# A mixer's hand-written order changed in three places: abs ahead of relu, low parts of turned blocks ahead of the softmax scaling, mean products a half projection behind their squares

## The chip, the core and the metric

The kernel runs on one core of a Trainium2 chip. Five engines run their own instruction streams and meet through semaphores: PE (TensorE: matrix products and turnings), ACT (ScalarE), DVE (VectorE), POOL (GpSimd) and SP (issues most DMAs). The metric is the device time of one execution in microseconds (us).

## What is computed

One encoder layer for one sequence of 512 positions and width 1024, in float32:

```python
h = modulate(x, g_ffn1, shift0, scale0);  x = x + 0.5 * gate0 * swiglu(h, w_ffn1_up, w_ffn1_down)
h = modulate(x, g_mix, shift1, scale1);   proj = h @ w_in          # q k v of 16 heads of 64, gates, forget logits
# 8 stick-breaking heads: z = q k^T / 8
log_beta = log_sigmoid(z); log_keep = where(strict, log_beta - z, 0)
w = where(strict, exp(log_beta + suffix_sum(log_keep)), 0);   o_sb = rmsnorm(w @ v)
# 8 forgetting heads: q, k = rmsnorm(q), rmsnorm(k)
p = softmax(where(causal, q k^T / 8 + f_cum[q] - f_cum[k], -inf));  o_fx = rmsnorm(p @ v) * sigmoid(gate)
x = x + gate1 * (concat(o_sb, o_fx) @ w_out)
h = modulate(x, g_ffn2, shift2, scale2);  x = x + 0.5 * gate2 * swiglu(h, w_ffn2_up, w_ffn2_down)
return rmsnorm(x, g_final)
```

## The kernel before

Every float32 product is made of three products of rounded parts: a high part (`_hi`, written by ACT) and the rest (`_lo`, written by DVE as value minus high part). So each weight tile of 128x1024 costs ACT one `w_hi` (L1107) and DVE one `w_lo` (L1471), and each product on PE is `three` (L694 to L696). Raw tiles arrive in four slots `w_raw`; SP loads a slot again once `w_lo_done` says that it was read. Split tiles have two slots.

The program is: first feed-forward block, mixer, output projection, second feed-forward block, final norm. The change lies in the mixer. It has eight jobs j of two heads: jobs 0 to 3 stick-breaking, 4 to 7 forgetting. A job has five units u of packed score blocks (128 x 512). A unit (j, u), numbered 5j+u, goes through these steps:

- `scores` on PE, into bank 2 or 3 (`bank[2 + unit % 2]`).
- `prep`. Stick-breaking: relu of the scores on DVE into `tmp_b` (L1839), and on ACT abs into `tmp_a` (L1374), exp (L1376), ln (L1378). Forgetting: on DVE the row maximum (L1849, negated at L1855), then on ACT the softmax exp with row sums (L1388).
- `sum`. Stick-breaking: on DVE the reversed scans (L1867) and a subtraction (L1871), then `exp` on ACT (L1394). Forgetting: reciprocal (L1878) and scaling (L1882) on DVE.
- `turn`: four 128x128 transposes on PE into bank 4 or 5 (L984).
- `unload`: high part `pt_hi` on ACT (L1402), low part `pt_lo` on DVE (L1889).
- `values`: once per job and head, the products of the turned blocks with v into bank 6 (L694 to L696 with `pt_hi` or `pt_lo` among the operands). Head 0 of job j is made in period u = 4 of job j, head 1 in period u = 1 of job j+1.

Beside them run the projections (`proj`, two halves per weight tile, 12 products 512 wide or 24 products 256 wide each), their evacuation (`evac`: q, k or v into high and low parts, or a gate's sigmoid in three ACT passes, L1303 to L1307), the splitting of weight tiles (`split`), the row of forget sums (`decay`, L1021 on PE, L1366 on ACT, through bank 7), and a chain of four steps per head norm: `square` on ACT into `ssum` (L1331); `stat`, the mean product on PE into bank 7 (L1012) with ln and exp on ACT (L1338, L1340); `scale` on DVE (L1804, for gated outputs L1809 too); `part`, high part on ACT (L1349, L1356, L1358) and low part on DVE (L1816, L1823, L1827). There are 16 norms: outputs of jobs 0 to 7, and q and k of jobs 4 to 7. Only one chain moves at a time.

The order of all this is fixed before the program is built, by `mixer_steps`. It walks through the 40 units; for each it runs through a string of letters, a period: `PERIOD[0]` for stick-breaking, `PERIOD[1]` for forgetting units. S is scores, P prep, U sum, E exp, T turn, L unload (T and L of the unit before), v values, d and D decay, a a half projection, b more of them if due, x the pending splits, m one step of the oldest norm chain, t one evacuation and one chain step. `LAG_STAT` holds a `stat` back until PE has been given so much work since the square; a half projection counts 12, scores 4, a turning 2. All engines then walk through the same list `STEPS`, each issuing its own part of every step, so the list sets the order within each engine; waits on semaphores set the rest.

Of the kernel before, what the change touches and what calls it, by code (L numbers as in the profile page):

```python
# [22 lines left out]
SBJ = 4  # L23
# [57 lines left out]

PERIOD = ("StPaamUdamvbtDTxxLxE", "SmPdaabTvtUtEamxDL")


LAG_STAT, LAG_BANK, LAG_TILE = 4, 1, 5
BEHIND = 18


# [5 lines left out]
def mixer_steps():  # L96
# [37 lines left out]
    def tick(force=False):  # L134

        if evacs:
            for b in banks_of(evacs[0][1]):
                since[b] = spent[0]
            emit(*evacs.pop(0))
        move(force)  # L140
# [75 lines left out]
    for p, (j, u) in enumerate(units):  # L216
        before = units[p - 1] if p else None
        due = min(total, halves_due(p))
        while u == 0 and any(step in made_first(j) for step in evacs + [chain[-1] for chain in chains]):
            tick(True)  # L220
        for item in PERIOD[0 if j < SBJ else 1]:
            if item == "S":
# [57 lines left out]
def hybrid_block_kernel(  # L280
# [4 lines left out]
    with ctx:  # L285
        def sem(name):
            return ctx.enter_context(nc.semaphore(name))
# [14 lines left out]
        def keep(name, shape, dt=F32):  # L302
# [127 lines left out]
        s_done, relu_done, abs_done, eneg_done, e_ready, scan_done, d_ready, p_ready_sb = (  # L430
            sem("s_done"), sem("relu_done"), sem("abs_done"), sem("eneg_done"), sem("e_ready"),
            sem("scan_done"), sem("d_ready"), sem("p_ready_sb"))
# [40 lines left out]
        def turned(u):  # L473

            if u in (0, 4):
                return [(u // 4, slice(3, 13, 3), slice(0, 4))]
            if u in (1, 3):
                return [(u // 3, slice(2, 9, 3), slice(0, 3)), (u // 3, slice(0, 1), slice(3, 4))]
            return [(0, slice(1, 5, 3), slice(0, 2)), (1, slice(1, 5, 3), slice(2, 4))]

        def blocks(b, which):
            return b[:].rearrange("p (b n) -> p b n", n=P)[:, which, :]
# [10 lines left out]
        def chunk_read(ci):  # L493

            what, n, _, _ = CHUNKS[ci]
            if what == "v":
                return v_ready, 2 * n + 2
            if what == "g":
                return g_copy, n - SBJ + 1
            if n < SBJ:  # L500
                return qk_ready, 2 * n + 1 + int(what == "k")
            return nrm_f32, norm_of(what, n) + 1
# [10 lines left out]
        def z_read(unit):  # L513

            return (d_ready, unit + 1) if unit < 5 * SBJ else (max_done, unit - 5 * SBJ + 1)
# [85 lines left out]
        def _(sp):  # L601
# [55 lines left out]
            for kind, n, _, tile in CHUNKS:  # L657
                if kind == "v":
                    c0 = (2 if n < 2 else 5) * 512 + (n % 2) * 256
                    for part in range(2):  # L660
                        t = tile + part
                        load_w(t, t % RAW, tile4(w_raw, t % RAW), in_v[:, 4 * part:4 * part + 4, c0:c0 + 256])
                else:
                    c0 = (3 * 512 if n >= SBJ else 0) + (n % SBJ) * P + {"q": 0, "k": 512, "g": 3 * 512}[kind]
                    load_w(tile, tile % RAW, tile8(w_raw, tile % RAW), in_v[:, :, c0:c0 + P])
# [23 lines left out]
        def _(pe):  # L689
# [202 lines left out]
            for step in STEPS:  # L892
                kind = step[0]
                if kind == "proj":
                    _, t, ci, half = step
                    what, n, b, first_tile = CHUNKS[ci]
                    if ci < 2:
# [191 lines left out]
        def _(act):  # L1089
# [176 lines left out]
            for step in STEPS:  # L1266
# [93 lines left out]
                elif kind == "decay":  # L1360
                    _, j, h = step
                    stats += 1
                    act.wait_ge(stat_done, stats)
                    if j > SBJ:
                        act.wait_ge(*z_read(5 * j - 1))
                    a(f_keys[:, h, :], bank[7][:], ACT.Copy).then_inc(stat_read, 1)  # L1366
                elif kind == "prep" and step[1] < SBJ:

                    unit = 5 * step[1] + step[2]
                    buf = tmp_a[:, unit % 2, :]  # L1370
                    act.wait_ge(relu_done, unit + 1)
                    if unit >= 2:
                        act.wait_ge(scan_done, unit - 1)
                    a(buf, bank[2 + unit % 2][:], ACT.Abs).then_inc(abs_done, 1)  # L1374
                    act.wait_ge(abs_done, unit + 1)
                    a(buf, buf, ACT.Exp, scale=-1.0).then_inc(eneg_done, 1)  # L1376
                    act.wait_ge(eneg_done, unit + 1)
                    a(buf, buf, ACT.Ln, bias=1.0).then_inc(e_ready, 1)  # L1378
                elif kind == "prep":

                    _, j, u = step
                    unit = 5 * j + u
                    buf = tmp_b[:, unit % 2, :]
                    fx = unit - 5 * SBJ
                    act.wait_ge(zf_ready, fx + 1)
                    for s, (h, i, c0) in enumerate(UNITS[u]):
                        seg = buf[:, c0:c0 + (i + 1) * P]
                        last = a(seg, seg, ACT.Exp, bias=small[:, 4 * (unit % 2) + s:4 * (unit % 2) + s + 1],  # L1388
                                 accum_out=small[:, 8 + 4 * (unit % 2) + s:9 + 4 * (unit % 2) + s])
                    last.then_inc(exp_done, 1)  # L1390
                elif kind == "exp" and step[1] < SBJ:
                    unit = 5 * step[1] + step[2]
                    act.wait_ge(d_ready, unit + 1)
                    a(tmp_b[:, unit % 2, :], tmp_b[:, unit % 2, :], ACT.Exp).then_inc(p_ready_sb, 1)  # L1394
                elif kind == "unload":
                    _, j, u = step
                    unit = 5 * j + u
                    act.wait_ge(t_done, unit + 1)
                    for h, dst, src in turned(u):
                        if j:  # L1400
                            act.wait_ge(pv_done, 2 * (j - 1) + h + 1)
                        last = a(pt_hi[:, h, dst, :], blocks(bank[4 + unit % 2], src), ACT.Copy)  # L1402
                    last.then_inc(pt_hi_done, 1)
# [59 lines left out]
        def _(dve):  # L1463
# [201 lines left out]
            with dve.Fori(0, UP_BLOCKS) as i:  # L1665
                for q in range(4):
                    f, j = 4 * i + 2 + q, q % 2
# [61 lines left out]
            for step in STEPS:  # L1729
# [101 lines left out]
                elif kind == "prep":  # L1831
                    _, j, u = step
                    unit = 5 * j + u
                    zb, buf = bank[2 + unit % 2], tmp_b[:, unit % 2, :]
                    dve.wait_ge(s_done, unit + 1)
                    if unit >= 2:
                        dve.wait_ge(t_done, unit - 1)
                    if j < SBJ:
# [18 lines left out]
                elif kind == "sum" and step[1] < SBJ:  # L1857

                    _, j, u = step
                    unit = 5 * j + u  # L1860
# [11 lines left out]
                elif kind == "sum":  # L1872
                    _, j, u = step
                    unit = 5 * j + u
# [9 lines left out]
                elif kind == "unload":  # L1884
                    _, j, u = step
                    unit = 5 * j + u
# [79 lines left out]
```

## Time and profile before

| | |
|---|---|
| runs | 1146.13 us median of 3 (1146.1 to 1147.53) |
| profiled execution | 1145.88 us, of which the profile spans 1144.1 us |
| PE busy | 1108.5 us, 97% |
| DVE busy | 596.1 us, 52% |
| ACT busy | 446.4 us, 39% |
| POOL busy | 71.7 us, 6% |

"Busy" counts an engine's own instructions, not waiting, branching or DMA issue. Matmuls overlap, so a PE that is busy is not thereby at its peak. A wait in the trace stands as idle time in front of an instruction, with the engine, tile and line that ended it.

### The profile page before, as it was taken

Reading aid. Unit: us, or ns where it says so; the run is one execution under the profiler, and the core shown is the slowest. Engines: PE = TensorE matmul, PEld = TensorE weight load, DVE = VectorE, ACT = ScalarE, POOL = GpSimd, SP = SyncE. Lnnn points to the kernel's source line nnn. Section 1 sums busy time; section 2 is a strip of 40 time slices with the busy share of each in tenths; the row PEclk is TensorE's granted clock in tenths of the full one; section 3 lists DMA queues with packets and bytes.
Section 4 is the critical chain, followed back from the end, with each engine's and each line's share of the span. In section 5 each row is a group of like instructions: output and inputs, shape, how many; then the busy total and the mean of one; then the engine's idle time right before and its main releaser. Section 6 shows DMA issues by size and latency. Waiting matters only on the chain.

```text
span 1144.1 us, 14298 instructions
## 1 busy us (share of the span) xinstructions
PE 1108.5 (97%) x5142; PEld 885.2 (77%) x5142; DVE 596.1 (52%) x829; ACT 446.4 (39%) x693; POOL 71.7 (6%) x68
## 2 busy tenths in 40 slices
PE   8999999999999999889999999999999999999997
PEld 5788888888788868678778767778888888878876
DVE  3746464655644556777766677663333333434343
ACT  5522222222222235566776665353222222312312
POOL 1000000000000001000000000000000000225350
PEclk9999999999999999999999999999999999999999
DMA  9755675565573631221212211332333333223221
GB/s 343 212 148 165 195 207 166 165 190 165 166 227 105 193 92 47 80 67 44 73 52 66 65 47 42 89 91 74 92 97 96 97 94 92 74 83 98 96 92 74
DMA packets 169687, 133.32 MB, mean 117 GB/s; under 512 B 5436, under 2 KB 150956, under 8 KB 169644
## 3 DMA queue, kind: packets, MB, share of 16 engines
q1 hardware_dynamic: 168704, 130.60, 38.0%
q0 software_dynamic: 768, 2.10, 0.8%
q8 instruction: 26, 0.43, 0.2%
q14 instruction: 17, 0.14, 0.0%
q10 hardware_dynamic: 172, 0.06, 0.0%
HBM read 128.54 MB, written 2.10 MB: 114 GB/s over the span
## 4 chain that ended last, share of the span: by engine, by line
PE 76%; DVE 12%; ACT 7%; issue 3%; DMA 1%; SPq 0%; DVEq 0%; ACTq 0%
PE bank L694 24%; PE bank L696 24%; PE bank L695 24%; DVE w_lo L1471 2%; DVE tmp_b L1867 2%; DVE pt_lo L1889 1%; PE bank L714 1%; ACT w_hi L1107 1%; ACT tmp_a L1376 1%; DVE tmp_b L1839 1%; ACT tmp_a L1374 1%; ACT tmp_a L1378 1%; DMA w_raw<-in_w_ffn_down_dram 1%; PE bank L1012 1%; DVE tmp_b L1871 1%
## 5 line engine op out<-in xcount | busy, mean ns | idle before, releaser
L1471 DVE TENSOR_TENSOR w_lo<-w_raw,w_hi 128x1024 fp32r<-128x1024 f32 x163 | 216.9, 1332 | 382.6 <-ACT w_hi L1107 382.1
L694 PE MATMUL bank<-h_hi,w_hi 128*128 128x512 f32 x864 | 349.2, 404 | 1.3 <-DVE v_lo L1772 0.3
L695 PE MATMUL bank<-h_lo,w_hi 128*128 128x512 f32 x864 | 342.9, 397 | 0.0
L696 PE MATMUL bank<-h_hi,w_lo 128*128 128x512 f32 x864 | 342.8, 397 | 0.0
L1107 ACT ACTIVATE w_hi<-w_raw 128x1024 fp32r<-128x1024 f32 x163 | 172.3, 1058 | 422.2 <-PE bank L696 402.5
L694 PEld LDWEIGHTS bank<-h_hi,w_hi 128*128 128x128 f32 x864 | 163.2, 189 | 44.9 <-issue 5.5
L695 PEld LDWEIGHTS bank<-h_lo,w_hi 128*128 128x128 f32 x864 | 163.1, 189 | 40.6 <-issue 2.6
L696 PEld LDWEIGHTS bank<-h_hi,w_lo 128*128 128x128 f32 x864 | 163.1, 189 | 39.6
L595 POOL TENSOR_TENSOR w_raw<-w_raw,gate_row 128x1024 f32<-128x1024 f32 (+1 forms) x24 | 54.9, 2287 | 378.9 <-DMA w_raw<-in_w_ffn_down_dram 378.6
L694 PE MATMUL bank<-w_hi,hid_hi 128*128 128x512 f32 x176 | 69.9, 397 | 3.2 <-DVE w_lo L1471 3.2
L694 PE MATMUL bank<-hid_hi,w_hi 128*128 128x512 f32 x176 | 70.1, 398 | 1.0 <-DVE w_lo L1471 1.0
L696 PE MATMUL bank<-w_hi,hid_lo 128*128 128x512 f32 x176 | 69.8, 396 | 0.0
L696 PE MATMUL bank<-hid_hi,w_lo 128*128 128x512 f32 x176 | 69.8, 396 | 0.0
L695 PE MATMUL bank<-hid_lo,w_hi 128*128 128x512 f32 x176 | 69.8, 396 | 0.0
L695 PE MATMUL bank<-w_lo,hid_hi 128*128 128x512 f32 x176 | 69.2, 393 | 0.0
L1483 DVE SCALAR_TENSOR_TENSOR ada_acc<-ada_w,cond,ada_acc 128x1024 f32<-128x1024 f32 x49 | 62.7, 1279 | 0.0
L1216 ACT ACTIVATE hid_hi<-tmp_b 128x512 f32 (+1 forms) x44 | 27.8, 632 | 85.6 <-DVE tmp_b L1663 81.1
L1598 DVE TENSOR_TENSOR hid_lo<-tmp_b,hid_hi 128x512 f32 (+1 forms) x44 | 30.5, 692 | 39.7 <-ACT hid_hi L1216 39.6
L1867 DVE TENSOR_TENSOR_SCAN tmp_b<-tmp_a,tmp_b 128x512 f32<-128x512 f32 (+3 forms) x32 | 25.1, 815 | 36.0 <-ACT tmp_a L1378 36.0
L694 PEld LDWEIGHTS bank<-w_hi,hid_hi 128*128 128x128 f32 x176 | 33.0, 188 | 11.7 <-DVE w_lo L1471 4.0
L694 PEld LDWEIGHTS bank<-hid_hi,w_hi 128*128 128x128 f32 x176 | 33.1, 188 | 9.3 <-DVE w_lo L1471 1.4
L696 PEld LDWEIGHTS bank<-hid_hi,w_lo 128*128 128x128 f32 x176 | 33.1, 188 | 8.1
(215 smaller groups left out, 1342.6 us busy)
## 6 DMA issues: line engine op xcount, KB each, us to landing
w_raw<-in_w_ffn_up_dram SPq DMA_DIRECT2D x88, 512.0 KB, 4.6
ada_w<-in_w_ada_dram SPq DMA_DIRECT2D x56, 512.0 KB, 3.6
w_raw<-in_w_ffn_down_dram SPq DMA_DIRECT2D x36, 512.0 KB, 4.4
w_raw<-in_w_in_dram SPq DMA_DIRECT2D x28, 512.0 KB, 3.7
ada_first<-in_w_ada_dram SPq DMA_DIRECT2D x16, 512.0 KB, 10.9
w_raw<-in_w_out_dram SPq DMA_DIRECT2D x8, 512.0 KB, 3.7
w_raw<-in_w_ffn_down_dram SPq DMA_DIRECT2D x8, 384.0 KB, 4.4
x_nat<-in_x_dram SPq DMA_DIRECT2D x4, 512.0 KB, 5.2
```

Source lines behind the costliest of these rows:

```text
L595: g.tensor_tensor(tile, tile, gate_row[:, :, half * 512:(half + 1) * 512] .broadcast_to([P, nk, 512]), ALU.mult).then_inc(w_gated, 1)
L694: mm(dst, wh, xh, start=start, stop=False, skip_group_check=skip)
L695: mm(dst, wh, xl, start=False, stop=False, skip_group_check=skip)
L696: return mm(dst, wl, xh, start=False, stop=stop, skip_group_check=skip)
L714: last = mm(bank[4 + p][:], cond[:, k:k + 1].broadcast_to([P, P]), ada_first[:, p, k, :], start=k == 0, stop=k == KC - 1)
L1012: mm(bank[7][:], pair_mean[:], ssum[:], start=True, stop=True).then_inc(stat_done, 1)
L1107: a(w_hi[:, s, :], w_raw[:, r, :], ACT.Copy).then_inc(w_hi_done, 1)
L1216: a(hid_hi[:, bass.ds(f, 1), :], tmp_b[:, j:j + 1, :], ACT.Copy).then_inc(hid_hi_done, 1)
L1471: v.tensor_tensor(w_lo[:, s, :], w_raw[:, r, :], w_hi[:, s, :].bitcast(F32), ALU.subtract)\
L1483: ins = v.scalar_tensor_tensor(ada_acc[:], source, cond[:, k:k + 1], ada_acc[:], ALU.mult, ALU.add)
L1598: v.tensor_tensor(hid_lo[:, bass.ds(f, 1), :], tmp_b[:, j:j + 1, :], hid_hi[:, bass.ds(f, 1), :].bitcast(F32), ALU.subtract).then_inc(hid_ ...
L1867: last = v.tensor_tensor_scan(buf[:, back], tmp_a[:, unit % 2, back], buf[:, back], 0.0, ALU.add, ALU.add)
```

## The change

In stick-breaking units ACT's abs no longer waits for DVE's relu but for the scores, and DVE's relu waits for abs. In the forgetting period the letter L moves from the end to right behind T: both halves of the unload of the unit before stand behind this unit's prep and ahead of its sum, on ACT and on DVE. And `LAG_STAT` goes from 4 to 12, so that a `stat` waits in the list until a half projection has been emitted behind its square. The number of instructions stays.

```diff
-PERIOD = ("StPaamUdamvbtDTxxLxE", "SmPdaabTvtUtEamxDL")
-LAG_STAT, LAG_BANK, LAG_TILE = 4, 1, 5
+PERIOD = ("StPaamUdamvbtDTxxLxE", "SmPdaabTvLtUtEamxD")
+LAG_STAT, LAG_BANK, LAG_TILE = 12, 1, 5
...
                     unit = 5 * step[1] + step[2]
                     buf = tmp_a[:, unit % 2, :]
-                    act.wait_ge(relu_done, unit + 1)
+                    act.wait_ge(s_done, unit + 1)
                     if unit >= 2:
                         act.wait_ge(scan_done, unit - 1)
                     a(buf, bank[2 + unit % 2][:], ACT.Abs).then_inc(abs_done, 1)
...
                     _, j, u = step
                     unit = 5 * j + u
                     zb, buf = bank[2 + unit % 2], tmp_b[:, unit % 2, :]
-                    dve.wait_ge(s_done, unit + 1)
+                    if j < SBJ:
+                        dve.wait_ge(abs_done, unit + 1)
+                    else:
+                        dve.wait_ge(s_done, unit + 1)
```

How the lists move, first on DVE in period (4,2), a forgetting period with the norm of output 3. Before:

```order
L1849 ISA tmp_b,small<-bank,f_keys 128x256
...
L1855 TENSOR_SCALAR small<-small 128x2
L1804 TENSOR_TENSOR nrm<-bank,rstd 128x512
L1878 RECIPROCAL small<-small 128x2
L1882 TENSOR_SCALAR tmp_b<-tmp_b,small 128x256 x2
L1816 SCALAR_TENSOR_TENSOR o_lo<-nrm,vcol,o_hi 128x512
L1471 TENSOR_TENSOR w_lo<-w_raw,w_hi 128x1024
L1889 TENSOR_TENSOR pt_lo<-bank,pt_hi 128x3x128
```

The same period now (three lines are added above, so L1852 is the maximum, L1885 the scaling, L1892 pt_lo):

```order
L1852 ISA tmp_b,small<-bank,f_keys 128x256
...
L1858 TENSOR_SCALAR small<-small 128x2
L1892 TENSOR_TENSOR pt_lo<-bank,pt_hi 128x3x128
...
L1881 RECIPROCAL small<-small 128x2
L1885 TENSOR_SCALAR tmp_b<-tmp_b,small 128x256 x2
L1804 TENSOR_TENSOR nrm<-bank,rstd 128x512
L1816 SCALAR_TENSOR_TENSOR o_lo<-nrm,vcol,o_hi 128x512
L1471 TENSOR_TENSOR w_lo<-w_raw,w_hi 128x1024
```

pt_lo went from last to second, and the norm's scaling from ahead of the softmax scaling to behind it.

On ACT in period (5,2), with the norm of output 4. Before:

```order
L1338 ACTIVATE rstd<-bank 128x512
L1340 ACTIVATE rstd<-rstd 128x512
L1388 ACTIVATE tmp_b,small<-tmp_b,small 128x256 x2
L1349 ACTIVATE o_hi<-nrm,vcol 128x512
L1331 ACTIVATE ssum<-bank 128x512
L1107 ACTIVATE w_hi<-w_raw 128x1024
L1402 ACTIVATE pt_hi<-bank 128x3x128
```

And now:

```order
L1331 ACTIVATE ssum<-bank 128x512
L1388 ACTIVATE tmp_b,small<-tmp_b,small 128x256 x2
L1402 ACTIVATE pt_hi<-bank 128x3x128
L1402 ACTIVATE pt_hi<-bank 128x128
L1338 ACTIVATE rstd<-bank 128x512
L1340 ACTIVATE rstd<-rstd 128x512
L1349 ACTIVATE o_hi<-nrm,vcol 128x512
L1107 ACTIVATE w_hi<-w_raw 128x1024
```

The norm's ln and exp stand behind the softmax exp and pt_hi instead of ahead of them, and the squares (here output 4's own) have come from the period before to the head of this one.

On PE around the same mean product, a piece of the difference (L984 is the turning of unit (5,1), L960 the next scores):

```order
+L694 MATMUL bank<-h_hi,w_hi 128x512
+L695 MATMUL bank<-h_lo,w_hi 128x512
...
+L984 MATMUL bank<-ident,tmp_b 128x128 x4
 L1012 MATMUL bank<-ssum,pair_mean 128x512
-L694 MATMUL bank<-h_hi,w_hi 128x512
-L695 MATMUL bank<-h_lo,w_hi 128x512
```

The half projection and the turning now stand ahead of the mean product instead of behind it.

## Rows read from the trace of the kernel before

**Rows 1.** Window: us; busy PE, PEld, DVE, ACT, POOL; PEclk, DMA share, GB/s

```profile
436.00:735.00 299.00, 279.42 (x1531) 228.47 (x1530) 206.76 (x401) 194.16 (x364) 10.52 (x20) 0.99 0.23 62
```

**Rows 2.** Waits of PE, 440 to 726 us: total, times, longest us

```profile
PE bank L694 <- DVE pt_lo L1889: 8.0, 4, 2.9
PE bank L1012 <- ACT ssum L1331: 5.0, 5, 2.0
```

**Rows 3.** Timelines, unit 2 (DVE, then ACT): start, us, what [idle before]

```profile
460.03 0.68 DVE L1839 TENSOR_SCALAR tmp_b<-bank 128x512 f32<-128x512 f32 x1
462.77 1.27 DVE L1867 TENSOR_TENSOR_SCAN tmp_b<-tmp_a,tmp_b 128x256 f32<-128x256 f32 x2 [2.06 <-ACT tmp_a L1378]
...
468.15 0.68 DVE L1839 TENSOR_SCALAR tmp_b<-bank 128x512 f32<-128x512 f32 x1
...
460.75 0.60 ACT L1374 ACTIVATE tmp_a<-bank 128x512 f32<-128x512 f32 x1 [2.74 <-DVE tmp_b L1839]
```

**Rows 4.** Granted clock (windows) and PE's timeline around 583 us

```profile
583.00:586.00 3.00, 3.00 (x9) 2.32 (x8) 2.25 (x5) 2.76 (x6) 0.00 (x0) 0.50 0.03 5
...
582.97 0.63 PE L695 MATMUL bank<-h_lo,w_hi 128*128 128x512 f32 x1
583.40 0.63 PE L696 MATMUL bank<-h_hi,w_lo 128*128 128x512 f32 x1
...
586.34 0.40 PE L694 MATMUL bank<-h_hi,w_hi 128*128 128x512 f32 x1
586.58 0.40 PE L695 MATMUL bank<-h_lo,w_hi 128*128 128x512 f32 x1
```

**Rows 5.** Timelines, period (6,0): ACT, DVE, then PE's mean product

```profile
657.11 1.05 ACT L1107 ACTIVATE w_hi<-w_raw 128x1024 fp32r<-128x1024 f32 x1
...
659.92 0.60 ACT L1338 ACTIVATE rstd<-bank 128x512 f32<-128x512 f32 x1 [0.73 <-PE bank L1012]
...
661.09 0.71 ACT L1388 ACTIVATE tmp_b<-tmp_b,small 128x512 f32<-128x512 f32 x1
...
661.95 1.46 ACT L1356 ACTIVATE q_st<-nrm,gq 64x512 fp32r<-64x512 f32 x2
663.43 0.60 ACT L1402 ACTIVATE pt_hi<-bank 128x512 fp32r<-128x512 f32 x1
...
658.19 1.22 DVE L1471 TENSOR_TENSOR w_lo<-w_raw,w_hi 128x1024 fp32r<-128x1024 f32 x1 [1.23 <-ACT w_hi L1107]
...
660.00 0.68 DVE L1849 CUSTOM_DVE_ANT_0 tmp_b<-bank,f_keys 128x512 f32<-128x512 f32 x1
...
661.22 0.69 DVE L1804 TENSOR_TENSOR nrm<-bank,rstd 128x512 f32<-128x512 f32 x1 [0.34 <-ACT rstd L1340]
...
662.19 0.49 DVE L1882 TENSOR_SCALAR tmp_b<-tmp_b,small 128x512 f32<-128x512 f32 x1
663.44 1.51 DVE L1823 SCALAR_TENSOR_TENSOR q_st<-nrm,gq,q_st 64x512 fp32r<-64x512 f32 x2 [0.76 <-ACT q_st L1356]
...
665.59 0.55 DVE L1849 CUSTOM_DVE_ANT_0 tmp_b<-bank,f_keys 128x384 f32<-128x384 f32 x1
...
658.79 1.10 PE L1012 MATMUL bank<-ssum,pair_mean 128*128 128x512 f32 x2 [0.97 <-ACT f_keys L1366]
```

**Rows 6.** PE's timeline, value product in period (1,1)

```profile
489.57 0.50 PE L694 MATMUL bank<-pt_hi,v_hi 128*128 128x512 f32 x1 [1.65 <-DVE pt_lo L1889]
```

**Rows 7.** PE's timeline: gate 5's projection, turnings, first product behind scores

```profile
598.57 0.47 PE L694 MATMUL bank<-h_hi,w_hi 128*128 128x512 f32 x1 [0.31 <-DVE nrm L1804]
...
632.77 0.60 PE L984 MATMUL bank<-ident,tmp_b 128*128 128x128 f32 x4
...
659.72 0.60 PE L984 MATMUL bank<-ident,tmp_b 128*128 128x128 f32 x4
...
660.85 0.48 PE L694 MATMUL bank<-h_hi,w_hi 128*128 128x512 f32 x1
...
709.84 0.60 PE L984 MATMUL bank<-ident,tmp_b 128*128 128x128 f32 x4
```

## Prediction

> **What bounds the kernel now.** The engine line of the page comes first: TensorE is busy nearly all the time, VectorE and ScalarE half of it or less (table above), so only TensorE's idle time can be won and only a new TensorE wait can cost. All that the diff moves lies in the mixer, 436 to 735 us. The window view gives TensorE 279.4 busy of 299 us there, VectorE 206.8, ScalarE 194.2 [rows 1]: 19.6 us is the most that vanishing waits can return, apart from clock. The waits say whose they are: 8.0 us for pt_lo before a value product, 5.0 for the squares before a mean product [rows 2].
>
> The timelines show why. In the stick-breaking half one round, from relu at 460.03 to relu at 468.15, is 8.1 us and a chain handed to and fro: ScalarE idles 2.74 us until relu has ended and abs may start, VectorE idles 2.06 until ScalarE's three passes are done [rows 3]. So in a round ScalarE has 5.4 us of work and VectorE 6.1. TensorE needs less than the round too: 24 products 0.235 apart, the spacing from 586.34 to 586.58 [rows 4], are 5.6; turning and the next scores are 1.1 (659.72 to 660.85 [rows 7]) to 1.4, in all 7.0. In the forgetting half nothing of the kind binds: a norm's ln and exp (from 659.92) are done before the softmax exp (661.09), VectorE's norm scaling (0.69) runs beside that exp, pt_hi follows at 663.43 and a new maximum at 665.59 [rows 5]. That round is 5.6 us, of which TensorE itself needs 4.6: a half projection 2.8, turning and scores 1.3, mean product 0.5.
>
> **Part 1, abs first.** No instruction is added or removed. Abs of unit p+1 can follow the exp of unit p on ScalarE, with relu beside ScalarE's next pass. The round then is the longer of two queues, 6.1 and 5.4, instead of their chain, and both are below TensorE's 7.0: TensorE bounds units 1 to 5. I replayed the queues from unit 0, every operation starting when its engine and its waits allow, with the durations of rows 3 to 5. The value product that stands at 489.57 behind a wait of 1.65 us [rows 6] starts at 481.3: **8.3 us earlier**. From there on v's low parts hold the next projection for 3 us, and at the value product of job 2 the lead is 7.7.
>
> **Part 2, mean products behind a half projection (LAG_STAT 12).** The waits for squares go, 5.0 us [rows 2]. But on ScalarE a norm's ln and exp now stand behind the unit's three passes (or behind its softmax exp), and VectorE's norm scaling behind the scan. Where norms follow period by period ScalarE idles during TensorE's half projection, and then TensorE waits for all that ScalarE still has to do. In job 3, from one mean product on: result 1.1, ln and exp 1.2, norm scaling 0.7, high parts 1.5, w_hi 1.05, pt_hi 0.6 [rows 5], exp 0.65, next squares 0.6 (passes as wide as pt_hi's), in all 7.4 us until the next mean product can start. TensorE has 4.6 us of work in that time: it waits about 3.0, twice, then 2.1 more before the decay row, which needs bank 7 read. Set against today's rounds there (6.8 to 7.7 us, the same waits and a slow clock in them) the lead shrinks to 3.7: **4.0 lost**. Then k5: its ln and exp stand behind the three passes of gate 4, so the projection of gate 5, on the same bank, starts near 599.0 instead of 598.57 [rows 7]: **4.2 lost**, the lead is gone.
>
> **Part 3, pt_lo between maximum and scaling.** pt_hi and pt_lo of unit p-1 need its turning, which stands on TensorE behind unit p's half projections. All that is queued behind them waits too: on VectorE the softmax scaling, the norm's scaling and low parts, w_lo and the next maximum; on ScalarE the norm's ln, exp and high parts and w_hi. Together with part 2 the round becomes one closed chain: maximum and softmax exp 2.0 to 2.1 (660.00 to 661.95 for a one-piece unit), pt_hi 0.65, pt_lo and softmax scaling 1.75 (ln and exp run beside them), norm scaling 0.7, high parts 1.46, low parts 1.51 [rows 5]: 8.2 us, and 1.25 more where a w_lo falls in; for a gated output, with one pass for two in the parts but one scaling more, 7.4 or 8.6. What part 3 removes is the wait of a value product for pt_lo, about 2 us in this half.
>
> Job 5 takes 26.95 us, from the last turning before it at 632.77 to its own at 659.72 [rows 7]. In the replay its maxima come 8.5, 9.0, 8.0 and 6.0 us apart, and TensorE waits at the turning of unit (5,2) 1.4, the next mean product 3.4 (its squares stand behind output 4's parts and a w_hi), the decay rows 2.5 and 1.4, the last turning 1.0. The job takes 34.2: **+7.3**. Jobs 6 and 7 take 50.1 us, to 709.84 [rows 7]. Job 6 has the same three norms and no projection in its first period (37.4 us, +8.9); job 7 has one norm, two gates and short output products that cover little of such a chain (30.8 us, +9.2): **+18.1**. Job 4, with one norm and a v projection held by v_lo, ends (632.77) at 636.6: **+3.3** on top.
>
> **The sum**: -8.3 + 0.6 + 4.0 + 4.2 + 3.3 + 7.3 + 18.1 = +29.2 us. Behind 710 us both programs have the same work, and the weight loads, which SP issues when w_lo of a slot is done, move along. **The clock** is the unknown. From 583 to 586 us the mean granted clock is 0.50, the 1.2 GHz level, and products start 0.43 apart (582.97, 583.40) instead of 0.235 [rows 4]; this is behind the longest wait for squares, 2.0 us [rows 2]. The mean of 0.99 over the mixer [rows 1] leaves room for one or two more such stretches, and eight products at 0.2 extra cost 1.6 each if TensorE sets the pace. The replay has none, but about ten waits of 2 us or more. Bounds: 0 and 16 us; most of them would fall where the other two engines set the pace, so I take the low end, 1.6. The profiled run took 1145.88 us (0.25 under the median of the runs): 1145.9 + 29.2 + 1.6 = **1176.7, rounded 1177 us**.
>
> The Trainium skill, "Perfetto Trace Analysis", section Identifying the Most-Contended Engine, has one judge Vector and Scalar by their occupancy and relieve the engine that is highest. By it two engines at 69% and 65% of this stretch have room, and all three moves only shorten TensorE's waits; that is rival 1.
>
> **Rivals.** 1, *faster: the spare time of VectorE and ScalarE swallows parts 2 and 3.* It decides whether a forgetting round with a norm stays at about 5.6 us. For: their shares, and the waits of rows 2 are those the edits aim at. Against: even today's round holds 0.76 us in which VectorE waits for high parts [rows 5], and a share says nothing of a closed chain. It returns 8.0 + 5.0 us and two clock stretches of 1.6: 1145.9 - 16.2 = 1130. Chance 0.10. 2, *slower by less: the lead of part 1 survives job 3 and k5,* because ScalarE reaches the norm passes before TensorE needs them: -7.7 + 3.3 + 7.3 + 18.1 = +21, and with half of job 7's loss covered by the output products +16: 1162. For: only two or three places decide it. Against: ScalarE's queue is in order. Chance 0.22. 3, *slower by more: the clock falls behind most of the new waits*: 1175.1 + 16 = 1191, or 1183 for half. Chance 0.14. 4, *no change*: part 1 pays for parts 2 and 3 to within 0.2%, about what a measurement of this kernel can tell from nothing: 0.03. The forecast itself has 0.51.
>
> The Trainium skill, "TensorE: Matmul & The Clock Gate", section Part 1, says that a gate halves the array's clock when the engine has been idle and gives it back when it is busy. By that rule rival 3 is what many new waits bring. The trace agrees in kind, with the 0.50; but the four waits for pt_lo, 2.0 us each in the mean, cannot all have brought a stretch at a mean clock of 0.99.
>
> The likeliest case alone spans 1168 to 1184, a quarter of the sum either way. The range takes in rivals 2 and 3 and leaves out 1: **1152 to 1190**. Faster by over 0.2%: 0.10; within: 0.03; slower: 0.87.
>
> **What would show it.** Right: the value product of 489.57 at 481 to 482; no wait of abs for relu; a v projection that waits some 3 us for v_lo; gate 5's projection waiting 4 to 5 us for the norm's scaling; maxima 8 to 9 us apart where a norm falls in a forgetting period; waits of 3 us before mean products and decay rows. Wrong: maxima 5 to 6 us apart in jobs 5 and 6, an end of the mixer before 735 us, or waits of TensorE there that sum to less than 20 us.

## The result and the profile after

| | before | after |
|---|---|---|
| runs | 1146.12 us median of 4 | 1171.64 us median of 4 (1170.69 to 1175.81) |
| profiled execution, its span | 1145.88, 1144.1 us | 1170.69, 1168.9 us |
| PE, DVE, ACT busy | 1108.5, 596.1, 446.4 us | 1117.2, 597.3, 446.0 us |

The ratio is 1.023, with a 95% interval of 1.0201 to 1.0258: the change is slower by 25.5 us. The profiled executions differ by 24.8.

The window view of the changed kernel, the mixer as a whole and then its two halves (columns as in [rows 1]):

```profile
436.00:760.00 324.00, 288.82 (x1535) 233.90 (x1534) 208.25 (x402) 193.98 (x364) 10.53 (x20) 0.96 0.22 58
436.00:590.00 154.00, 142.72 (x826) 119.45 (x825) 113.82 (x164) 107.36 (x184) 7.43 (x14) 0.99 0.26 67
590.00:760.00 170.00, 146.10 (x711) 114.45 (x710) 94.44 (x240) 86.62 (x180) 3.09 (x6) 0.93 0.18 49
```

The mixer's work took 299 us before [rows 1] and takes 324 now. DVE and ACT do the same work as before (208.3 and 194.0). PE has 35.2 us of idle time instead of 19.6, so 15.6 of the 25 are idle time. The other 9.4 are longer PE busy time for the same products, and most of that is the clock: its mean is 0.96 instead of 0.99, and 0.93 in the second half. An estimate of its share from the two traces: set against the spacing of the same two products where the granted clock is full, the products that start at the lower level take 11.0 us longer in the change and 3.0 before, 7.9 more.

The waits of PE, 440 to 751 us (total, times, longest, in us):

```profile
PE bank L1012 <- ACT ssum L1331: 8.5, 4, 2.8
PE bank L984 <- DVE tmp_b L1885: 6.9, 9, 1.3
PE bank L694 <- DVE nrm L1804: 5.4, 2, 4.4
PE bank L694 <- DVE v_lo L1772: 4.3, 3, 2.1
PE bank L1021 <- ACT rstd L1338: 4.1, 3, 2.1
PE bank L694 <- DVE pt_lo L1892: 1.9, 1, 1.9
PE bank L694 <- DVE o_lo L1816: 1.7, 1, 1.7
PE bank L694 <- DVE k_l_a L1792: 1.2, 1, 1.2
```

Against [rows 2], the wait for pt_lo has gone from 8.0 to 1.9. The wait for squares, which the late mean product should have removed, has risen from 5.0 to 8.5: in fewer places, but longer. Five kinds of wait that were small or absent have come up beside them: the turning for the softmax scaling, a projection for a norm's scaling, v_lo, the decay row for bank 7, an output product for o_lo.

PE's timeline after, at the places of [rows 6, 7]: the value product of period (1,1), gate 5's projection, the turnings (4,4), (5,4) and (7,4).

```profile
481.17 0.40 PE L694 MATMUL bank<-pt_hi,v_hi 128*128 128x512 f32 x1
...
598.37 0.76 PE L694 MATMUL bank<-h_hi,w_hi 128*128 128x512 f32 x1 [4.43 <-DVE nrm L1804]
...
636.74 0.60 PE L984 MATMUL bank<-ident,tmp_b 128*128 128x128 f32 x4
...
669.74 0.66 PE L984 MATMUL bank<-ident,tmp_b 128*128 128x128 f32 x4 [0.88 <-DVE tmp_b L1885]
...
734.47 0.66 PE L984 MATMUL bank<-ident,tmp_b 128*128 128x128 f32 x4 [0.97 <-DVE tmp_b L1885]
```

The value product starts 8.4 us earlier (489.57 before). The turning (4,4) is 4.0 us late, (5,4) 10.0, (7,4) 24.6. So the gain is made in the first 55 us of the mixer, is lost by 600 us, and what stays as loss at the end is made from there on.

What sets the pace there is one round from maximum to maximum. Before, the maxima of units (5,2) and (5,3) are 6.9 us apart:

```profile
641.95 0.41 DVE L1849 CUSTOM_DVE_ANT_0 tmp_b<-bank,f_keys 128x256 f32<-128x256 f32 x1
...
648.82 0.55 DVE L1849 CUSTOM_DVE_ANT_0 tmp_b<-bank,f_keys 128x384 f32<-128x384 f32 x1
```

DVE and then ACT in the period of unit (5,2), with the norm of output 4, in the changed kernel:

```profile
649.30 0.42 DVE L1852 CUSTOM_DVE_ANT_0 tmp_b<-bank,f_keys 128x256 f32<-128x256 f32 x1
...
651.98 0.76 DVE L1892 TENSOR_TENSOR pt_lo<-bank,pt_hi 128x384 fp32r<-128x384 f32 x2 [1.70 <-ACT pt_hi L1402]
...
652.85 0.62 DVE L1885 TENSOR_SCALAR tmp_b<-tmp_b,small 128x256 f32<-128x256 f32 x2
653.38 0.68 DVE L1804 TENSOR_TENSOR nrm<-bank,rstd 128x512 f32<-128x512 f32 x1
654.10 0.69 DVE L1809 TENSOR_TENSOR nrm<-nrm,sig 128x512 f32<-128x512 f32 x1
655.64 0.75 DVE L1816 SCALAR_TENSOR_TENSOR o_lo<-nrm,vcol,o_hi 128x512 fp32r<-128x512 f32 x1 [0.86 <-ACT o_hi L1349]
656.52 1.22 DVE L1471 TENSOR_TENSOR w_lo<-w_raw,w_hi 128x1024 fp32r<-128x1024 f32 x1
657.66 0.55 DVE L1852 CUSTOM_DVE_ANT_0 tmp_b<-bank,f_keys 128x384 f32<-128x384 f32 x1
...
650.32 0.51 ACT L1388 ACTIVATE tmp_b<-tmp_b,small 128x256 f32<-128x256 f32 x1 [2.04 <-DVE small L1858]
...
651.32 0.63 ACT L1402 ACTIVATE pt_hi<-bank 128x384 fp32r<-128x384 f32 x2
651.85 0.59 ACT L1338 ACTIVATE rstd<-bank 128x512 f32<-128x512 f32 x1
652.47 0.63 ACT L1340 ACTIVATE rstd<-rstd 128x512 f32<-128x512 f32 x1
654.82 0.72 ACT L1349 ACTIVATE o_hi<-nrm,vcol 128x512 fp32r<-128x512 f32 x1 [1.72 <-DVE nrm L1809]
655.45 1.04 ACT L1107 ACTIVATE w_hi<-w_raw 128x1024 fp32r<-128x1024 f32 x1
656.39 0.58 ACT L1331 ACTIVATE ssum<-bank 128x512 f32<-128x512 f32 x1
```

Read it as one line that crosses between the engines: maximum 649.30, softmax exp, pt_hi 651.32, pt_lo 651.98, two scalings, the gate's product, o_hi 654.82, then w_hi and w_lo, the next maximum 657.66. That is 8.4 us. Each engine shows idle time in brackets, and yet neither can start anything earlier, since each works through its own list in order. The squares at 656.39 are the last item of ACT's half, and the mean product at 657.02 has waited 2.85 us for them (that row stands with the clock at the end).

### The profile page after: what moved, and what is told of

It reads as the page before. It is cut to its first block, busy times and chain, and to the rows that moved or that the text cites. A ratio compares the mean times of both kernels' runs of the same rounds, so it can differ in the third digit from the quotient of the medians.

```text
span 1168.9 us, 14304 instructions
## 1 busy us (share of the span) xinstructions
PE 1117.2 (96%) x5142; PEld 890.5 (76%) x5142; DVE 597.3 (51%) x829; ACT 446.0 (38%) x693; POOL 71.6 (6%) x68
## 4 chain that ended last, share of the span: by engine, by line
PE 77%; DVE 11%; ACT 6%; issue 4%; DMA 2%; SPq 0%; DVEq 0%; ACTq 0%
PE bank L694 24%; PE bank L696 24%; PE bank L695 24%; DVE w_lo L1471 2%; ACT w_hi L1107 1%; DVE pt_lo L1892 1%; PE bank L714 1%; DVE tmp_b L1870 1%; DMA w_raw<-in_w_ffn_down_dram 1%; ACT pt_hi L1402 1%; DVE tmp_b L1852 1%; DVE nrm L1804 1%; PE bank L984 1%; DMA x_nat<-in_x_dram 1%; PE bank L1012 1%
## 5 line engine op out<-in xcount | busy, mean ns | idle before, releaser
L694 PE MATMUL bank<-h_hi,w_hi 128*128 128x512 f32 x864 | 348.2, 403 | 7.9 <-DVE nrm L1804 5.4
L694 PEld LDWEIGHTS bank<-h_hi,w_hi 128*128 128x128 f32 x864 | 164.5, 190 | 48.5 <-issue 9.6
L694 PE MATMUL bank<-w_hi,hid_hi 128*128 128x512 f32 x176 | 69.9, 397 | 3.1 <-DVE w_lo L1471 3.1
L694 PE MATMUL bank<-hid_hi,w_hi 128*128 128x512 f32 x176 | 70.1, 399 | 1.6 <-DVE w_lo L1471 1.6
L1892 DVE TENSOR_TENSOR pt_lo<-bank,pt_hi 128x128 fp32r<-128x128 f32 (+2 forms) x64 | 29.1, 486 | 47.4 <-ACT pt_hi L1402 47.3
L694 PEld LDWEIGHTS bank<-w_hi,hid_hi 128*128 128x128 f32 x176 | 33.0, 188 | 11.7 <-DVE w_lo L1471 4.0
L694 PEld LDWEIGHTS bank<-hid_hi,w_hi 128*128 128x128 f32 x176 | 33.2, 188 | 9.9 <-DVE w_lo L1471 2.1
L694 PE MATMUL bank<-w_hi,h_hi 128*128 128x256 f32 x128 | 36.7, 287 | 3.3 <-DVE v_lo L1772 2.1
```

The lines of the kernel that those rows point to most:

```text
L694: mm(dst, wh, xh, start=start, stop=False, skip_group_check=skip)
L1892: last = v.tensor_tensor(pt_lo[:, h, dst, :], blocks(bank[4 + unit % 2], src), pt_hi[:, h, dst, :].bitcast(F32), ALU.subtract)
```

## The experiments

All were timed in three rounds beside the kernel before, which gave medians of 1145.2 to 1145.9 us in them.

**The three parts, alone and in pairs.** Part 1 is abs first, part 2 is `LAG_STAT` 12, part 3 the early unload. Each kernel takes the lines of the change that belong to its parts:

```diff
# part 1 (e1, e4, e5)
-                    act.wait_ge(relu_done, unit + 1)
+                    act.wait_ge(s_done, unit + 1)
...
-                    dve.wait_ge(s_done, unit + 1)
+                    dve.wait_ge(abs_done if j < SBJ else s_done, unit + 1)
# part 2 (e3, e5, e6)
-LAG_STAT, LAG_BANK, LAG_TILE = 4, 1, 5
+LAG_STAT, LAG_BANK, LAG_TILE = 12, 1, 5
# part 3 (e2, e4, e6)
-PERIOD = ("StPaamUdamvbtDTxxLxE", "SmPdaabTvtUtEamxDL")
+PERIOD = ("StPaamUdamvbtDTxxLxE", "SmPdaabTvLtUtEamxD")
```

Expected of part 1 alone:

> Part 1 alone (abs ahead of relu). Chain theory: the stick-breaking rounds of units 1 to 5 fall from 8.1 to about 7 us, the value product of 489.57 us comes near 481, the forgetting half is as before; 6 to 10 us faster (ratio 0.991 to 0.995). Rival, spare capacity: the same stretch gains and the waits for squares in the forgetting half stay; no difference between the two here. Rival, that relu as second reader costs VectorE what ScalarE gains: within 2 us of before.

Expected of part 3 alone:

> Part 3 alone (L behind T in the forgetting period). Chain theory: ln and exp of a norm still stand ahead of the softmax exp, so the round is about 7 us instead of 5.6 to 6.9; the change costs 5 to 10 us. Additive rival, part 3 the culprit: it costs 20 us or more alone, since everything on VectorE stands behind the turning. Spare-capacity rival: it gains 1 to 2 us, the waits of value products for pt_lo in this half.

Expected of part 2 alone:

> Part 2 alone (LAG_STAT 12). Chain theory: job 3 and the wait of gate 5's projection for k5's scaling cost 6 to 8 us, the forgetting rounds with a norm some more; in all 8 to 15 us slower, the waits for squares gone or moved. Additive rival: about 25 less what part 3 costs, plus what part 1 gains, so that the three single runs sum to +25. Spare-capacity rival: 3 to 5 us faster, the waits for squares gone.

Expected of parts 1 and 3:

> Parts 1 and 3 (LAG_STAT stays 4). Chain theory: the sum of the two alone, 0 to 3 us either side of before, since they act in different halves; and it is 20 us or more faster than all three parts, since the closed round needs the late mean product. Additive rival: all three parts minus the cost of part 2 alone.

Expected of parts 1 and 2:

> Parts 1 and 2 (L stays at the period's end). Chain theory: the lead of part 1 is used up in job 3 and at gate 5's projection; the forgetting rounds with a norm are about 7.8 us instead of 8.2 to 9.4; 5 to 12 us slower than before. Additive rival: exactly the sum of the two single runs. If part 1 gains less here than alone by 4 us or more, the lead is lost to the same waits (no additivity).

Expected of parts 2 and 3:

> Parts 2 and 3 (relu first as before). Chain theory: more than the two single runs together by 5 us or more (closed round), and since the lead of part 1 is used up at gate 5's projection anyway, it is only 0 to 4 us slower than all three parts: 1171 to 1176. Additive rival: slower than all three by all that part 1 gains alone (about 8 us), 1180.

Measured, with the ratio to before and its 95% interval:

| | without part 1 | with part 1 |
|---|---|---|
| neither 2 nor 3 | 1146.1 | e1: 1130.7 us, 0.9873 (0.9857 to 0.989) |
| part 3 | e2: 1180.9 us, 1.0301 (1.028 to 1.0323) | e4: 1165.3 us, 1.0179 (1.0162 to 1.0196) |
| part 2 | e3: 1185.8 us, 1.035 (1.0331 to 1.0368) | e5: 1163.2 us, 1.0149 (1.0132 to 1.0166) |
| both | e6: 1194.2 us, 1.0416 (1.0399 to 1.0434) | the change: 1171.6 us, 1.023 |

**Part 1 alone is the fastest version timed: it beats both kernels, by 15 us and by 41.** Parts 2 and 3 cost 32 and 35 us beside it, each on its own, and 41 together. Part 1 itself is worth some 15 us alone and beside part 3, and 22.6 beside part 2, with part 3 or without.

None of the six times of the chain theory was met. I had the costs of the singles well below these, because I took the closed chain for the work of both together, and the gain of part 1 too low. Of the rivals only one holds, that part 3 alone costs 20 us or more (e2).

The times of the turnings say where. The table gives the start of PE's L984 against before, in us (before: 604.26 for (4,0), 709.84 for (7,4)):

| turning | after | e1 | e2 | e3 | e4 | e5 | e6 |
|---|---|---|---|---|---|---|---|
| (4,0) | +2.3 | -14.9 | +2.0 | +24.7 | -12.0 | +1.0 | +26.9 |
| (7,4) | +24.6 | -14.9 | +35.9 | +41.1 | +18.7 | +17.5 | +49.2 |
| between | 22.3 | 0.0 | 33.9 | 16.4 | 30.7 | 16.5 | 22.3 |

Part 1 makes its 14.9 us before (4,0) and nothing behind it. Part 2 costs 15.9 us before (4,0) beside part 1 (e5 against e1) and 24.7 alone, and 16.4 to 16.5 behind it. Part 3 costs 2 to 3 us before (4,0) and 31 to 34 behind it; but where it is there, adding part 2 takes 8 to 12 us off that half (30.7 to 22.3, 33.9 to 22.3). So the costs of 2 and 3 neither add up nor need each other.

That part 2 costs 8.8 us less before (4,0) where part 1 stands beside it is in good part the clock. By the estimate used above, the products at the lower level take 12.7 us longer there in e3 against 3.0 in the kernel before, and 4.8 in e5 against none in e1: 4.9 of the 8.8. PE's waits for pt_lo, up to 4.0 us in e3, are at most 1.9 in e5.

**Why part 2 alone closes the round.** The same round in e5, which has the unload at the period's end (DVE, then ACT):

```profile
648.04 0.41 DVE L1849 CUSTOM_DVE_ANT_0 tmp_b<-bank,f_keys 128x256 f32<-128x256 f32 x1
...
651.32 0.69 DVE L1804 TENSOR_TENSOR nrm<-bank,rstd 128x512 f32<-128x512 f32 x1 [0.33 <-ACT rstd L1340]
...
655.61 0.75 DVE L1889 TENSOR_TENSOR pt_lo<-bank,pt_hi 128x384 fp32r<-128x384 f32 x2
656.27 0.55 DVE L1849 CUSTOM_DVE_ANT_0 tmp_b<-bank,f_keys 128x384 f32<-128x384 f32 x1
...
650.04 0.58 ACT L1338 ACTIVATE rstd<-bank 128x512 f32<-128x512 f32 x1
...
652.77 0.72 ACT L1349 ACTIVATE o_hi<-nrm,vcol 128x512 fp32r<-128x512 f32 x1 [1.48 <-DVE nrm L1809]
653.40 1.04 ACT L1107 ACTIVATE w_hi<-w_raw 128x1024 fp32r<-128x1024 f32 x1
654.34 0.64 ACT L1402 ACTIVATE pt_hi<-bank 128x384 fp32r<-128x384 f32 x2
654.87 0.60 ACT L1331 ACTIVATE ssum<-bank 128x512 f32<-128x512 f32 x1
```

From 648.04 to 656.27 are 8.2 us, with nearly the same items in another order: here ln and exp stand behind the softmax exp, and pt_hi is last instead of first. The kernel before does ln and exp beside the maximum, ahead of the softmax exp [rows 5]. So part 2 closes the round by itself; that is shown. Which of its moves does it is read from the rows and was not tested: part 2 puts the squares behind the scores, the mean product with ln and exp behind the half projection, and the norm's scaling behind the softmax scaling, all at once.

The distances between the maxima of units (5,1) to (6,0), in us, tell the kernels apart:

| | (5,1) to (5,2) | to (5,3) | to (5,4) | to (6,0) |
|---|---|---|---|---|
| before, and e1 | 5.7 | 6.9 | 5.7 | 5.5 |
| the change | 8.7 | 8.4 | 7.9 | 5.4 |
| e5, parts 1 and 2 | 9.7 | 8.2 | 7.8 | 5.5 |
| e4, parts 1 and 3 | 7.3 | 9.6 | 9.0 | 5.4 |

**Why part 3 alone is dearer in that half.** In e4 the mean product stands right behind the scores, ahead of the half projection. PE, ACT and DVE in the period of unit (6,2):

```profile
675.34 0.60 PE L984 MATMUL bank<-ident,tmp_b 128*128 128x128 f32 x4
...
675.98 0.66 ACT L1402 ACTIVATE pt_hi<-bank 128x384 fp32r<-128x384 f32 x2 [2.53 <-PE bank L984]
...
676.67 0.76 DVE L1889 TENSOR_TENSOR pt_lo<-bank,pt_hi 128x384 fp32r<-128x384 f32 x2 [4.83 <-ACT pt_hi L1402]
677.34 0.68 DVE L1804 TENSOR_TENSOR nrm<-bank,rstd 128x512 f32<-128x512 f32 x1
...
678.78 0.72 ACT L1349 ACTIVATE o_hi<-nrm,vcol 128x512 fp32r<-128x512 f32 x1 [2.15 <-DVE nrm L1809]
...
679.41 0.58 ACT L1331 ACTIVATE ssum<-bank 128x512 f32<-128x512 f32 x1
...
680.04 1.12 PE L1012 MATMUL bank<-ssum,pair_mean 128*128 128x512 f32 x2 [3.38 <-ACT ssum L1331]
...
685.35 0.60 PE L984 MATMUL bank<-ident,tmp_b 128*128 128x128 f32 x4
```

This is a loop through PE itself: turning, pt_hi, pt_lo, the norm's scaling, o_hi, the next squares, mean product (4.7 us), and behind it the half projection (5.3 us, most of its products at half clock, 0.43 apart) up to the next turning: 10.0 us. Both other engines stand idle for the turning, 2.53 and, through pt_hi, 4.83 us. With part 2 in, the half projection stands ahead of the mean product and runs beside these steps. That would account for the 8 to 12 us that part 2 gives back in this half; it is read from the rows, no run tests it alone.

**Which item behind pt_lo costs.** Three kernels with part 1 and a part 3 in steps. e7 moves ACT's half of the unload alone (a step of its own, "high", at the new letter H):

```diff
-PERIOD = ("StPaamUdamvbtDTxxLxE", "SmPdaabTvtUtEamxDL")
+PERIOD = ("StPaamUdamvbtDTxxLxE", "SmPdaabTvHtUtEamxDL")
...
-                elif kind == "unload":
+                elif kind == "high":
```

> Base is abs first alone (1130.7 us). Added: in forgetting periods only ScalarE's half of the unload (pt_hi) moves up behind the turning; VectorE's pt_lo stays at the period's end. The whole move cost 35 us (1165.3). Theory A, VectorE's queue is what costs (softmax scaling, norm scaling, low parts and the next maximum all stand behind pt_lo, and pt_lo waits for a turning that stands behind a half projection): with pt_lo late nearly nothing is lost, 1131 to 1138. Theory B, ScalarE's queue is what costs (squares, ln and exp, parts and w_hi stand behind a pt_hi that waits for the turning, and the mean product waits for the squares): most of the 35 stays, 1150 to 1165, with waits of 3 us before mean products.

Measured 1140.3 us, 0.9953 (0.9936 to 0.9969): 9.6 us over e1, in neither band. ACT's half alone costs a quarter of part 3; the other 25 us come when DVE's half moves too (DVE's half alone was not timed). PE's wait for squares goes from 3.0 us in 4 places (e1) to 7.0 in 7. Theory A named the larger half; that ACT's would cost nearly nothing was wrong.

e8 and e10 keep both halves together and move them less far:

```diff
-PERIOD = ("StPaamUdamvbtDTxxLxE", "SmPdaabTvtUtEamxDL")
+PERIOD = ("StPaamUdamvbtDTxxLxE", "SmPdaabTvtULtEamxD")   # e8: behind the softmax scaling
+PERIOD = ("StPaamUdamvbtDTxxLxE", "SmPdaabTvtLUtEamxD")   # e10: behind the norm's scaling only
```

> Base is abs first alone (1130.7 us). Added: in forgetting periods both halves of the unload move up, but only to right behind the softmax scaling (the sum step), one letter behind the place that cost 35 us (1165.3). VectorE's scaling of the softmax and of the norm then stand ahead of pt_lo; the parts, w_hi and w_lo behind it. Theory A1, the link that costs is the scaling behind pt_lo (the next turning waits for it, a loop through TensorE): 1131 to 1142. Theory A2, what costs is that parts, splits and the next maximum stand behind the unload, whatever stands ahead: 1152 to 1165.

> Base is abs first alone (1130.7 us). Added: in forgetting periods both halves of the unload stand behind the norm's scaling but still ahead of the softmax scaling; behind both it cost 1.5 us (1132.2), ahead of both 34.6 (1165.3). Theory A, the link that costs is the softmax scaling (the next turning reads it, so turning, pt_hi, pt_lo, scaling, turning is a loop, and the scaling stands in it in every period): 1155 to 1165. Theory B, the link is the norm's scaling with the norm's parts behind it (periods with a norm alone): 1131 to 1140.

e8: 1132.2 us, 0.9888 (0.9872 to 0.9905), within 1.5 us of e1. e10: 1137.6 us, 0.9926 (0.9909 to 0.9942). So of the 34.6 us of part 3, having the unload in front of the norm's scaling makes 27.7 (1165.3 to 1137.6), and in front of the softmax scaling 5.4. The 27.7 hold some clock too: by the estimate above slow products take 8.7 us longer in e4 and nothing in e10. This decides for the norm: theory B of the e10 run. The theory that the softmax scaling is the loop, which e8 seemed to bear out, has fallen as the main cause. In e10 the mean product of the period of unit (6,2) waits 1.12 us, not 3.38, for o_hi no longer stands behind pt_lo:

```profile
660.63 0.69 DVE L1804 TENSOR_TENSOR nrm<-bank,rstd 128x512 f32<-128x512 f32 x1
...
662.90 0.72 ACT L1349 ACTIVATE o_hi<-nrm,vcol 128x512 fp32r<-128x512 f32 x1
663.12 0.76 DVE L1889 TENSOR_TENSOR pt_lo<-bank,pt_hi 128x384 fp32r<-128x384 f32 x2 [1.07 <-ACT pt_hi L1402]
...
664.16 1.12 PE L1012 MATMUL bank<-ssum,pair_mean 128*128 128x512 f32 x2 [1.12 <-ACT ssum L1331]
```

**The same letters beside part 2.** e11 and e12 are the change with the unload further back:

```diff
-PERIOD = ("StPaamUdamvbtDTxxLxE", "SmPdaabTvLtUtEamxD")
+PERIOD = ("StPaamUdamvbtDTxxLxE", "SmPdaabTvtULtEamxD")   # e11: behind the softmax scaling
+PERIOD = ("StPaamUdamvbtDTxxLxE", "SmPdaabTvtUtLEamxD")   # e12: behind the norm's scaling too
```

> Base is the change itself (1171.6 us); part 1 with part 2 alone is 1163.2. The unload moves from ahead of the softmax scaling to behind it; abs first and the late mean products stay. Theory A, only the scaling behind pt_lo is a cost of part 3: with that gone the time is that of parts 1 and 2, 1161 to 1166. Theory B, my closed chain (norm scaling, parts and next maximum behind pt_lo, in periods where the mean product comes late) is what sets job 5 to 7: 1167 to 1172, maxima still over 8 us apart in job 5.

> Base is the change itself (1171.6 us; parts 1 and 2 alone 1163.2). The unload moves behind both scalings, ahead of the norm's parts and the splits. Theory A: with the late mean product a norm's ln, exp, scaling, parts and w_hi, w_lo all run between one softmax exp and the next maximum, wherever the unload stands among them; so the round of units (5,2) and (6,2) stays a closed chain of over 8 us, turnings (5,2) to (5,3) stay some 12 us apart, and the time is that of parts 1 and 2, 1161 to 1166. Theory B: in parts 1 and 2 the chain runs through pt_hi, which stands behind the parts and w_hi there; with pt_hi ahead of them it opens: turnings (5,2) to (5,3) 7 to 9 us apart, 1150 to 1158.

e11: 1170.2 us, 1.0209 (1.0192 to 1.0226), theory B. With the late mean product the norm's scaling is emitted by the t behind U, so "ULt" puts the unload ahead of it all the same. The place that cost 1.5 us in e8 costs 7.0 here (1163.2 to 1170.2), nearly all of the 8.4 that part 3 costs beside parts 1 and 2. e12: 1156.5 us, 1.0099 (1.008 to 1.0117), 15 us less than the change and 6.7 less than parts 1 and 2 with the unload last (e5). Turnings (5,2) to (5,3) are 9.7 us apart there (649.56 to 659.27), 12.4 in e5 and 12.0 in the change. So beside part 2 pt_hi and pt_lo are cheapest, of the places timed, where they fill the engines' waits for each other, between the norm's scaling and its parts. Without part 2 the period's end is as good or better (e8 is 1.5 us behind e1). The time falls into the band of theory B, the distance of 9.7 misses it by 0.7: the round is shorter, not open. From unit (5,2) on its maxima are 7.6 and 7.0 us apart, where before they were 6.9 and 5.7.

**Gate 5's projection.** e9 is the change with one swap in the list, the mean product of k5 ahead of gate 4's evacuation (seven lines are added above, so L694 is L701 there):

```diff
     def tick(force=False):
+        if chains and chains[0][0][0] == "stat":
+            move(force)
...
+            return
```

```text
-turn 3 4; unload 3 4; evac g4; stat k5; sum 4 0; scale k5
+turn 3 4; unload 3 4; stat k5; evac g4; sum 4 0; scale k5
```

> Base is the change itself (1171.6 us). One swap in the list: in period (4,0) the mean product of k5 with its ln and exp stands ahead of the evacuation of gate 4 (three passes on ScalarE), not behind. Theory A, ScalarE's queue order is why gate 5's projection waits 4.4 us at 598.37 for the norm's scaling: ln and exp come 1.8 us (three passes of 0.6) or more earlier, the wait falls to between 1 and 2.6 us, the half-clock stretch behind it goes or shortens, 1167 to 1170 in all. Theory B, the norm scaling is late for other reasons (VectorE's softmax scaling and pt_lo stand ahead of it): wait and time stay within 0.5 us, 1171 to 1172.

Measured 1164.9 us, 1.0169 (1.0152 to 1.0186), 6.8 under the change by the medians and 2 us below the band of theory A. In e9, gate 5's projection:

```profile
595.54 0.47 PE L701 MATMUL bank<-h_hi,w_hi 128*128 128x512 f32 x1 [1.72 <-DVE nrm L1811]
```

The wait falls from 4.43 to 1.72 us, as theory A has it, and the turning (4,0) comes 5.37 us earlier, at 601.23. 2.8 of these are there when the projection starts (595.54 instead of 598.37), nearly all by the shorter wait. The other 2.5 come behind it, and they are the clock: behind the wait of 4.43 the change makes 12 products 0.43 apart, e9 none there. The lead stays at 5.3 us up to the turning (7,4).

## Why the prediction was right, and where it was not

The forecast was 1177 us in a range of 1152 to 1190, slower with 0.87. It came out at 1171.6. The positions of PE, against before, as the working had them and as the trace of the change has them:

| place | predicted | measured |
|---|---|---|
| value product (1,1) | -8.3 (481.3) | -8.4 (481.17) |
| value product of job 2 | -7.7 | -8.2 |
| turning (3,4), behind job 3's norms | -3.7 | -5.2 |
| turning (4,0), behind gate 5's wait | +0.5 | +2.3 |
| turning (4,4) | +3.8 (636.6) | +4.0 (636.74) |
| job 5 alone | +7.3 | +6.0 |
| job 6 alone | +8.9 | +7.7 |
| job 7 alone | +9.2 | +6.9 |

The near match at (4,4) is luck: on the way there four terms miss by 0.5, 1.0, 3.3 and 1.7 us, and cancel.

**Part 1.** The mechanism is right: no abs waits for relu, relu comes every 6.1 us (459.07, 465.17 in the change), and v's low parts hold a projection for 2.1 us where 3 was forecast. The 8.3 us hold for the place in the changed kernel, and are wrong as the worth of the part, which is 14.9 us alone and 22.6 beside part 2. In e1 the lead is 10.2 us at the turning (1,1), 12.0 at (2,3) and 14.9 at (3,3), which is behind the place of [rows 4], where e1 has no product at half clock. I had it end at 8.3, and what it can still gain in jobs 2 and 3 without part 2 stands nowhere in my sum.

**Part 2.** The two places of the stick-breaking half were named rightly, job 3 and gate 5. In job 3 the mean products were to wait 3.0 twice and the decay row 2.1; they wait 0.98, 1.85 and 1.17, and the loss there is 3.0 instead of 4.0. At gate 5 the wait was to be 4 to 5 us and is 4.43, but the loss from (3,4) to (4,0) is 7.5 instead of 4.2: 5.0 up to the start of the projection, and 2.5 behind it, where the 12 half-clock products stand. That "the waits for squares go" was wrong: they are 8.5 us, since the squares themselves come late. And part 2 was charged with nothing of its own behind the turning (4,4), where e5 shows some 15 us.

**Part 3.** The round was to have its maxima 8.5, 9.0, 8.0 and 6.0 us apart in job 5. They are at 640.58, 649.30, 657.66, 665.54 and 670.91: 8.7, 8.4, 7.9 and 5.4. Of the waits at its end the mean product's was to be 3.4 and is 2.85, the first decay row's 2.5 and is 2.14, the last turning's 1.0 and is 0.88, while turning (5,2) was to wait 1.4 and waits 0.47 and the second decay row waits for nothing. With such overshoots jobs 5 and 6 were put 1.2 us too long each and job 7 2.3: 4.8 us, close to the 5.1 between 1176.7 and the result. The rounds of the three jobs are the term of the sum that was mis-sized. One overshoot can be read off: pt_lo with the softmax scaling was put at 1.75 us and takes 1.40 (651.98 to 653.38). In the trace neighbours on one engine overlap a little, as pt_hi of two pieces and ln do, which start 0.53 us apart (651.32, 651.85) while pt_hi ends after 0.63.

The step that failed is the sentence "together with part 2 the round becomes one closed chain". Each part closes it alone (e4, e5). The total came out well because the replay walked the true list with both edits in it, whatever sentence I set above it. What I forecast by these words for part 2 or part 3 alone was too low by 25 us or more each (e3: 8 to 15 us, measured 40; e2: 5 to 10, measured 35).

**The clock.** I took 1.6 us with bounds of 0 and 16. In the change 35 products of 512 columns in projections start 0.43 us apart, in four stretches, against the 8 of [rows 4] before. Over products of every width it is the 7.9 us given with the result. One such stretch is shown to cost its full length, at gate 5; what the others cost was not measured on its own. So this term was put too low (gate 5 alone has 2.5), and the 29.2 us of the queues too high, for the 24.6 at turning (7,4) hold the clock as well. The two errors have opposite signs and made the total look better than its parts: that, too, is luck.

**The rivals.** Rival 1, spare time that swallows parts 2 and 3, is out: ACT and DVE are busy 51% and 56% of the window from 590 to 760 us and set its pace. The Trainium skill, "Perfetto Trace Analysis", section Identifying the Most-Contended Engine, would have one optimize the most contended engine first, and judge PE's headroom by MFU (its products against its peak) and by weight loads rather than by how long matmuls are busy. By weight loads as by matmuls (67% and 86% of this window) that is PE. The trace agrees that PE bounds the kernel, but what the edits cost came of PE's waits for the two engines with the lower shares, and of the clock behind these waits. The time of rival 1, 1130, came of part 1 alone, by another way. Rival 2, that the lead survives job 3 and gate 5, fell at gate 5; of job 3 5.2 of the 8.2 us did survive. Rival 3, a lower clock behind most of the new waits, came in kind and not in size: the change has five waits of 2 us or more, not some ten, and the lower level stands in or behind four of them, for 7.9 us instead of 16. (Its 1191 lay just outside the range that was said to take it in.) "No change" is outside the interval.

## What to carry to other kernels

Busy shares don't tell whether an engine that works through a fixed list has room. Walk the list from one instance of an operation to its next, across all engines, and see whether the chain closes; then ask of each single edit whether it closes the chain without the others, for the cost of two edits that each close a chain in the same round is neither their sum nor shared out between them. Put a step that waits for another engine where its own engine would wait anyway (e12's place for the unload) and behind the step that other engines wait for (the norm's scaling, e10), and measure every part of a change alone: here one of three parts was worth 15 us and the other two hid it.

## What the runs showed of the hardware

The granted clock falls to the 1.2 GHz level behind some waits of PE and not behind others of nearly the same length. Windows of the changed kernel over two such stretches, and the PE rows ahead of them:

```profile
659.00:666.00 7.00, 5.16 (x18) 4.08 (x19) 4.00 (x9) 3.85 (x10) 1.03 (x2) 0.76 0.35 93
688.00:701.00 13.00, 9.41 (x25) 6.37 (x26) 7.82 (x19) 7.06 (x16) 1.03 (x2) 0.61 0.24 62
```

```profile
657.02 1.13 PE L1012 MATMUL bank<-ssum,pair_mean 128*128 128x512 f32 x2 [2.85 <-ACT ssum L1331]
660.84 0.50 PE L1021 MATMUL bank<-f_cum,rowsel 128*128 128x512 f32 x1 [2.14 <-ACT rstd L1338]
...
690.83 2.07 PE L1012 MATMUL bank<-ssum,pair_mean 128*128 128x512 f32 x2 [2.85 <-ACT ssum L1331]
```

Behind the first wait of 2.85 us the mean product still runs in 1.13 us, and products go 0.43 apart from 662.2 on, behind a second wait of 2.14. Behind the other, the same wait in the same place of the next job, the mean product itself takes 2.07, and the slow spacing lasts to 699.1. In e12 both of these waits are 2.70, and the mean granted clock from 600 to 760 us is 1.00. So 0.15 us less of waiting, with what lies around it, went with 17 slow products fewer. The length of the wait alone does not decide: in e4 the projection of gate 5 waits 1.98 us (585.04) and 7 products behind it go 0.43 apart, in e12 and e5 the same projection waits 2.77 us (598.82, 599.60) and none does. What else decides stays open here.

The second thing that I had not expected is how much of a queue's cost the clock can carry. A swap that shortened one wait by 2.7 us brought 5.4 at the next turning, since the slow stretch behind it went too (e9).
